# Encoder step on one core: the MLP as seven quarter products (one level of Strassen's algorithm) in place of the plain tiled product

## The chip, the core and the metric

The kernel runs on one core of a Trainium2 chip. TensorE (PE in the profile) multiplies, VectorE (DVE), ScalarE (ACT) and GpSimd (POOL) do elementwise work, and the queue of SyncE (SP) issues the transfers. The metric is the device time of one execution in microseconds, lower is better.

## The reference

Two post-norm layers are run over 1024 prompt rows and 32 sample rows, D = 1024, all in fp32. Each layer has attention, an output projection and then the MLP, the part that the change rewrites:

```python
x = layer_norm(ALPHA * x + g1 * (o @ w_out)) * ln1_g + ln1_b
u = layer_norm(x) * (1 + sc2) + sh2
f = jnp.square(jax.nn.relu(u @ w1)) @ w2        # w1 (1024, 4096), w2 (4096, 1024)
x = layer_norm(ALPHA * x + g2 * f) * ln2_g + ln2_b
```

## The kernel before

Activations lie transposed: features on the 128 partitions, the T = 1056 tokens along the free axis. TensorE is given fp32r operands: every fp32 operand x is split into hi = round(x) and lo = x - hi, and a product is three passes, hi·hi, lo·hi and hi·lo, added in PSUM (`three_pass`, L370).

The MLP of a layer runs in a block of its own (L2068). The 4096 hidden features are walked in 16 blocks of 256. `up` makes the two 128-row tiles of a block (8 depths x 3 passes x 3 column blocks of NB = 352), `down` multiplies the block before into all 8 output tiles (2 depths x 3 passes x 3 column blocks). That is 4608 matmuls of 352 columns for a layer. What the other engines do for a block of 256 features:

- POOL: `pool_split` (L349) makes hi (L356) and lo (L358) of two 1 MB weight chunks of 128x2048, and lo (L2083) of two hidden tiles of 128x1056.
- ACT: relu out of PSUM (L2136) and the rounded hidden tile (L2138), 128x1056, twice each.
- DVE: the square of a hidden tile (L2146), twice, and the scaled sum of each of 8 output tiles from PSUM into `acc` (L2163, three instructions a tile).

The first `up` block of a layer is fed while rows are turned: `turned_feed` (L423) transposes one depth at a time on TensorE, ACT scales and shifts it (`read_turned_rows`, L458), DVE splits it (`split_turned_rows`, L473: L496 hi, L498 lo) and TensorE multiplies it (L452). Ahead of the MLP block stands the block of the output projection and the first norm (L1922), behind it the block of the second norm (L922 or L2177): there `rows_back` (L814) turns `acc` back into rows (L821), and between its tiles the products for the next layer's conditioning run (`pe_chunks`, L603), whose first three weight chunks are loaded at the end of the MLP block. Engines meet at a barrier between blocks. Within a block each engine runs its own instruction list in order and waits on semaphores. `Own.settle` makes an engine wait for its own last instruction.

## Time and profile before

| what | value |
|---|---|
| median of 3 runs | 3213.33 us (3211.71 to 3226.49) |
| profiled execution, first to last instruction (the one time that its profile gives) | 3228.2 us |
| PE busy over the span | 2944.9 us, 91% |
| DVE busy | 1630.8 us, 51% |
| ACT busy | 871.7 us, 27% |
| POOL busy | 1514.3 us, 47% |
| mean granted TensorE clock | 0.930 |
| matmul instructions | 18646 |

A busy share says how long an engine had an instruction running, blocked ones included, averaged over stages that have different limits. Read it stage by stage. A matmul's listed duration overlaps its neighbours'; what one costs in a stream is the distance between starts.

### The profile page before, as it was taken

How to read it: one execution, taken by the hardware profiler on the slowest of the kernel's cores; microseconds unless marked ns; L12 is line 12 of the kernel's file. 1: busy time of each engine (PE TensorE's matmuls, PEld its weight loads, DVE VectorE, ACT ScalarE, POOL GpSimd, SP SyncE). 2: the span in 40 equal slices, each digit the busy share in tenths (PEclk: the TensorE clock that was granted, in tenths of full speed). 3: DMA queues.
4: the chain of work that ended last, by engine and by line, in shares of the span. 5: the costliest groups of instructions: out<-in, count | busy, mean ns of one | idle time of the engine just before them, and what ended most of it. 6: DMA issues, size and time to landing. Idle time of an engine off the chain costs nothing. (4 is left out here: it accounts for less than half of the span.)

```text
span 3228.2 us, 47279 instructions
## 1 busy us (share of the span) xinstructions
PE 2944.9 (91%) x18646; PEld 2808.2 (87%) x18646; DVE 1630.8 (51%) x3479; ACT 871.7 (27%) x1710; POOL 1514.3 (47%) x680
## 2 busy tenths in 40 slices
PE   5999899887999999999979989987979999999993
PEld 5999789565899999999979888985859999999993
DVE  6552688557423332333775418875654333333347
ACT  1331466325200010001253306663251110011001
POOL 2693596125334343444339727742334343434334
PEclk6999999889999999999779998997989999999996
DMA  5451211421111111110534412114211111111112
GB/s 227 161 170 54 79 41 44 140 90 71 66 40 52 39 52 39 52 39 26 214 144 157 159 37 58 45 39 151 95 65 40 53 39 52 39 51 39 52 40 94
DMA packets 117355, 253.65 MB, mean 79 GB/s; under 512 B 42565, under 2 KB 78953, under 8 KB 103701
## 3 DMA queue, kind: packets, MB, share of 16 engines
q1 hardware_dynamic: 110868, 228.58, 20.8%
q10 hardware_dynamic: 6336, 23.07, 2.0%
q8 instruction: 94, 1.54, 0.2%
q14 instruction: 57, 0.46, 0.0%
HBM read 217.19 MB, written 42.19 MB: 80 GB/s over the span
## 5 line engine op out<-in xcount | busy, mean ns | idle before, releaser
L377 PE MATMUL psum<-u_hi,w_hi 128*128 128x352 f32 x2016 | 651.4, 323 | 4.0 <-DVE v_rows L1240 4.0
L377 PE MATMUL psum<-u_lo,w_hi 128*128 128x352 f32 x2016 | 652.4, 324 | 0.0
L377 PE MATMUL psum<-u_hi,w_lo 128*128 128x352 f32 x2016 | 651.5, 323 | 0.0
L2163 DVE SCALAR_TENSOR_TENSOR acc_t<-psum,mods,acc_t 128x704 f32<-128x704 f32 x720 | 376.2, 578 | 275.0 <-PE psum L377 275.0
L377 PE MATMUL psum<-h_hi,w_lo 128*128 128x352 f32 x1536 | 495.3, 322 | 0.0
L377 PE MATMUL psum<-h_lo,w_hi 128*128 128x352 f32 x1536 | 495.0, 322 | 0.0
L377 PE MATMUL psum<-h_hi,w_hi 128*128 128x352 f32 x1536 | 494.3, 322 | 0.0
L356 POOL CAST w_hi<-w_raw 128x2048 fp32r<-128x2048 f32 x72 | 136.3, 1894 | 659.0 <-DVEq L2156 357.4
L2146 DVE TENSOR_TENSOR h_relu<-h_relu 128x1056 f32<-128x1056 f32 x64 | 112.2, 1753 | 634.3 <-ACT h_relu L2136 634.3
L377 PEld LDWEIGHTS psum<-u_hi,w_hi 128*128 128x128 f32 x2016 | 379.9, 188 | 5.2 <-issue 5.0
L377 PEld LDWEIGHTS psum<-u_lo,w_hi 128*128 128x128 f32 x2016 | 380.2, 189 | 0.0
L377 PEld LDWEIGHTS psum<-u_hi,w_lo 128*128 128x128 f32 x2016 | 379.6, 188 | 0.0
L2136 ACT ACTIVATE h_relu<-psum 128x1056 f32<-128x1056 f32 x64 | 67.4, 1052 | 1102.4 <-PE psum L377 1094.8
L358 POOL TENSOR_TENSOR w_lo<-w_raw,w_hi 128x2048 fp32r<-128x2048 f32 x72 | 359.0, 4986 | 5.8
L1067 POOL TENSOR_TENSOR ada_products<-w_ada_b,c_rows 128x1024 f32<-128x1024 f32 x88 | 238.5, 2742 | 128.6 <-DVE u_lo L498 97.2
L2083 POOL TENSOR_TENSOR h_lo<-h_relu,h_hi 128x1056 fp32r<-128x1056 f32 x64 | 158.1, 2471 | 283.0 <-ACT h_hi L2138 273.4
L377 PEld LDWEIGHTS psum<-h_hi,w_hi 128*128 128x128 f32 x1536 | 289.4, 188 | 0.0
L377 PEld LDWEIGHTS psum<-h_lo,w_hi 128*128 128x128 f32 x1536 | 289.1, 188 | 0.0
L377 PEld LDWEIGHTS psum<-h_hi,w_lo 128*128 128x128 f32 x1536 | 288.5, 188 | 0.0
L1474 PE MATMUL psum<-v_parts,probs_hi 128*128 128x128 f32 x840 | 204.3, 278 | 10.0 <-DVE o_head L1584 8.1
L1474 PE MATMUL psum<-v_parts,probs_lo 128*128 128x128 f32 x840 | 207.9, 282 | 0.0
L675 POOL TENSOR_TENSOR row_tiles<-row_tiles,ln_gain 128x1024 f32<-128x1024 f32 x32 | 76.1, 2377 | 249.5 <-ACT row_tiles L701 249.5
(267 smaller groups left out, 5724.0 us busy)
## 6 DMA issues: line engine op xcount, KB each, us to landing
w_raw<-in_w_all SPq DMA_DIRECT2D x86, 1024.0 KB, 4.8
w_ada_b<-in_w_ada_t ACTq DMA_DIRECT2D x44, 512.0 KB, 3.5
w_ada_v<-in_w_ada_t SPq DMA_DIRECT2D x20, 512.0 KB, 3.3
row_tiles<-in_x_prompt SPq DMA_DIRECT2D x16, 512.0 KB, 13.6
scr_o<-o_head SPq DMA_DIRECT2D x32, 256.0 KB, 2.6
row_tiles<-scr_o SPq DMA_DIRECT2D x16, 512.0 KB, 16.3
x_between_norms<-row_tiles SPq DMA_DIRECT2D x16, 512.0 KB, 2.6
mlp_rows<-x_between_norms SPq DMA_DIRECT2D x16, 512.0 KB, 6.9
```

The lines of the kernel that those rows point to most:

```text
L356: pool.tensor_copy(hi[:, 0:c], raw[s][:, 0:c]).then_inc(pool_step, 1)
L358: pool.tensor_tensor(lo[:, 0:c], raw[s][:, 0:c], hi[:, 0:c].bitcast(F32), ALU.subtract).then_inc(pool_step, 1)
L377: mm = pe.matmul(out[:, b, :], w[s][:, c:c + P], a[:, k, b * NB:(b + 1) * NB], start=(k == 0 and w is w_hi and a is a_hi), stop=(k == n - ...
L675: own.did(pool.tensor_tensor(x, x, ln_g[:], ALU.mult))
L1067: pool.tensor_tensor(ada_prod[c][:], ada_b[i % 2][:], c_rows[:, c, :], ALU.mult).then_inc(b_prod, 1)
L1474: mm = pe.matmul(psum[:, 6 + n % 2, 0:2 * HD], p[n % 2][:, b, :], v, start=(b == 0 and p is pt_hi), stop=(b == nb - 1 and p is pt_lo))
L2083: pool.tensor_tensor(h_lo[par][:, m, :], h_r[m][:], h_hi[par][:, m, :].bitcast(F32), ALU.subtract).then_inc(h_rdy, 1)
L2136: act.activation(h_r[m][:].rearrange("p (b c) -> p b c", c=NB), lin[m], ACT.Relu).then_inc(h_ev[m], 1)
L2146: dve.tensor_tensor(h_r[m][:], h_r[m][:], h_r[m][:], ALU.mult).then_inc(h_sqd, 1)
L2163: ins = dve.scalar_tensor_tensor(a, y, mods[:, 40 + m, c:c + 1], a, ALU.mult, ALU.add)
```

## The change

Both matrices of a layer's MLP are cut in 2x2 quarters, group by group: the hidden features are taken in SB = 4 groups of 1024. For a group, `up` is a product of a 1024x1024 piece of w1 with u and `down` one of a 1024x1024 piece of w2 with the hidden piece. Either is done as the seven products M1 to M7 of Strassen's algorithm, on 512x512 weight quarters and 512x528 token quarters. That makes 56 steps (`STEPS`), numbered g, a layer: `UP_ORDER` and `DOWN_ORDER` four times. A step has four output tiles m, each two column blocks of 264 x 4 depths x 3 passes: 96 matmuls of 264 columns. Operands that are sums of two quarters are summed in fp32 by DVE (`weight_sum`, `token_sum`), then rounded by ACT (`weight_high`, `token_high`); the rest is subtracted by POOL (`weight_low`, and `token_low` for depths 0 and 1) and by DVE (`token_low` for depths 2 and 3). Token parts are double buffered, half weight parts (index q = 2g, 2g+1) have three buffers. A sum shares its buffer with the low part that replaces it. A product's tile is added into one or two quarters of the hidden piece or of `acc`. The gate `g2` is applied once at the end of a layer (`gate`) and no longer in each sum. The weights are loaded as quarters of 1 MB, four a matrix.

The loads of the first two quarters stand in the block ahead, where POOL no longer splits the first chunk. `mlp_x` is now loaded behind the last `up` step, and the three conditioning chunks (`ada_r`) behind the last product. The diff, cut to its core and with leading blanks taken off (the transposes' `turn_depth` is as `turned_feed`'s, two PSUM pairs in turn; `evict` calls `evict_up` or `evict_down`; `gate` is four to six scaled copies of an output tile on ACT):

```diff
+SB = 4
+HT = KT // 2
+TH = 528
+NH2 = TH // 2
+UP_ORDER = ("M7", "M1", "M2", "M4", "M6", "M5", "M3")
+DOWN_ORDER = ("M2", "M4", "M5", "M3", "M7", "M1", "M6")
+PER = len(UP_ORDER)
+STEPS = [(s, half, name) for s in range(SB) for half, names in (("up", UP_ORDER), ("down", DOWN_ORDER)) for name in names]
+NSTEP = len(STEPS)
+CHAIN_HEAD = ("M7", "M2", "M5", "M6")
+WEIGHT_OF = {"M1": ((0, 0), (1, 1), 1), "M2": ((1, 0), (1, 1), 1), "M3": ((0, 0), None, 0), "M4": ((1, 1), None, 0),
+             "M5": ((0, 0), (0, 1), 1), "M6": ((1, 0), (0, 0), -1), "M7": ((0, 1), (1, 1), -1)}
+TOKEN_OF = {"M1": ((0, 0), (1, 1), 1), "M2": ((0, 0), None, 0), "M3": ((0, 1), (1, 1), -1), "M4": ((1, 0), (0, 0), -1),
+            "M5": ((1, 1), None, 0), "M6": ((0, 0), (0, 1), 1), "M7": ((1, 0), (1, 1), 1)}
...
-mlp_x = at("mlp_rows", U0, [P, NTT, D])
-ada_r = [at(f"w_ada_r{s}", U0 + 36864 + 8192 * s, [P, CW]) for s in range(3)]
+mlp_x = at("mlp_rows", W0 + 87040, [P, NTT, D])
+ada_r = [at(f"w_ada_r{s}", W0 + 53248 + 8192 * s, [P, CW]) for s in range(3)]
...
+m_raw = {q: at(f"w_quarter{i}", W0 + 8192 * i, [P, 2, D]) for i, q in enumerate(QUADS)}
+m_whi = [at(f"w_part_hi{s}", W0 + 32768 + 4096 * s, [P, D], F32R) for s in range(3)]
+lo_at = (W0 + 45056, W0 + 49152, Q0 + 83200)
+m_wlo = [at(f"w_part_lo{s}", o, [P, D], F32R) for s, o in enumerate(lo_at)]
+m_wsum = [at(f"w_part_sum{s}", o, [P, D]) for s, o in enumerate(lo_at)]
+m_thi = [at(f"token_part_hi{s}", W0 + 53248 + 16896 * s, [P, HT, TH], F32R) for s in range(2)]
+m_tlo = [at(f"token_part_lo{s}", W0 + 61696 + 16896 * s, [P, HT, TH], F32R) for s in range(2)]
+m_tsum = [at(f"token_part_sum{s}", W0 + 61696 + 16896 * s, [P, HT, TH]) for s in range(2)]
+m_u = at("mlp_in", W0 + 87040, [P, KT, T])
+m_h = at("mlp_hidden", Q0 + 40960, [P, KT, T])
+m_rest = at("mlp_rest", Q0 + 74752, [P, HT, TH])
...
-sp_weights(sp, l, UP0, 1)
+sp.wait_ge(raw_free, UP0 + 1)
+load_quarter(sp, l, 0, (1, 1))
+sp.wait_ge(raw_free, UP0 + 2)
+load_quarter(sp, l, 0, (0, 1))
...
-pool.wait_ge(f_last, USE + 1)
-pool_weights(pool, UP0, 1)
...
+sp.wait_ge(n_tlo_p, g + 1 + HT // 2 - 1)
+sp.wait_ge(n_tlo_v, g)
 mlp_rows_loaded(sp, 0, NTT)
 if l + 1 < DEPTH:
+    sp.wait_ge(n_mm, HT * NSTEP)
     sp_chunks(sp, l + 1, 0, 3)
...
+x = m_wsum[s][:] if b else m_raw[a][:, j, :]
+pool.wait_ge(n_whi, q + 1)
+pool.tensor_tensor(m_wlo[s][:], x, m_whi[s][:].bitcast(F32), ALU.subtract).then_inc(n_wlo, 1)
...
+pool.wait_ge(n_thi, g)
+pool.tensor_tensor(m_tlo[s][:, 0:2, :], x[:, 0:2, :], m_thi[s][:, 0:2, :].bitcast(F32), ALU.subtract)\
+    .then_inc(n_tlo_p, 1)
...
+for g in range(1, NSTEP):
+    if g == 1:
+        weight_low(2)
+        token_low(1)
+    else:
+        token_low(g)
+        weight_low(2 * g)
+    weight_low(2 * g + 1)
...
+def product(g, m):
+    name = STEPS[g][2]
+    first = name in CHAIN_HEAD
+    if m == 0:
+        pe.wait_ge(n_tlo_p, g + HT)
+        if g > 0:
+            pe.wait_ge(n_tlo_v, g)
+    if m % 2 == 0:
+        pe.wait_ge(n_wlo, 2 * g + m // 2 + 1)
+    if g > 0:
+        if ACT_EV[g] > ACT_EV[g - 1]:
+            pe.wait_ge(n_eva, HT * ACT_EV[g - 1] + m + 1)
+        if DVE_EV[g] > DVE_EV[g - 1]:
+            pe.wait_ge(n_evv, HT * DVE_EV[g - 1] + m + 1)
+    s, w = parity(g), half_slot(2 * g + m // 2)
+    for b in range(2):
+        for k in range(HT):
+            c = 256 * k + P * (m % 2)
+            for a, t in ((m_whi, m_thi), (m_wlo, m_thi), (m_whi, m_tlo)):
+                mm = pe.matmul(banks(m)[:, b, :], a[w][:, c:c + P], t[s][:, k, NH2 * b:NH2 * b + NH2],
+                               start=(first and k == 0 and a is m_whi and t is m_thi),
+                               stop=(k == HT - 1 and t is m_tlo), skip_group_check=not first)
+    mm.then_inc(n_mm, 1)
...
+for i in range(6):
+    turn_depth(i)
+product(0, 0)
+turn_depth(6)
+pe.wait_ge(n_rows, 1)
+product(0, 1)
+turn_depth(7)
+pe.wait_ge(n_feed, 8)
+product(0, 2)
+product(0, 3)
...
+act.activation(m_thi[parity(g)][:], x, ACT.Copy).then_inc(n_thi, 1)
...
+func = ACT.Copy if name in ("M7", "M1") else ACT.Relu
+own.did(act.activation(split_two(out), banks(m), func), n_eva)
+if func is ACT.Relu:
+    own.settle()
+    own.did(act.activation(out, out, ACT.Square), n_sq)
...
+for g in range(1, NSTEP):
+    if g >= 2:
+        evict(g - 2, 3)
+    token_high(g)
+    if g >= 2:
+        weight_high(2 * g)
+    evict(g - 1, 0)
+    evict(g - 1, 1)
+    weight_high(2 * g + 1)
+    evict(g - 1, 2)
+for m in range(HT):
+    gate(m)
...
+def weight_sum(q):
+    g, j = q // 2, q % 2
+    a, b, sign = WEIGHT_OF[STEPS[g][2]]
+    if not b:
+        return
+    quarters_ready(dve, g)
+    if q >= 3:
+        dve.wait_ge(n_mm, HT * ((q - 3) // 2) + 2 * ((q - 3) % 2) + 2)
+    own.did(dve.tensor_tensor(m_wsum[half_slot(q)][:], m_raw[a][:, j, :], m_raw[b][:, j, :],
+                              ALU.add if sign > 0 else ALU.subtract), n_wsum)
+def token_sum(g):
+    s, half, name = STEPS[g]
+    a, b, sign = TOKEN_OF[name]
+    if not b:
+        return
+    if g >= 2:
+        dve.wait_ge(n_mm, HT * (g - 1))
+    if half == "down":
+        own.settle()
+        dve.wait_ge(n_sq, 2 * HT * s + (HT if name == "M4" else 2 * HT))
+    x = source(g)
+    own.did(dve.tensor_tensor(m_tsum[parity(g)][:], quarter_of(x, a), quarter_of(x, b),
+                              ALU.add if sign > 0 else ALU.subtract), n_tsum)
...
+dve.wait_ge(n_thi, g)
+own.did(dve.tensor_tensor(m_tlo[s][:, 2:4, :], x[:, 2:4, :], m_thi[s][:, 2:4, :].bitcast(F32),
+                          ALU.subtract), n_tlo_v)
...
+def accumulate(dst, m, op, first, done):
+    if first:
+        ins = dve.tensor_copy(split_two(dst), banks(m))
+    else:
+        own.settle()
+        ins = dve.tensor_tensor(split_two(dst), split_two(dst), banks(m), op)
+    own.did(ins, done)
+def relu_square(x, done):
+    own.settle()
+    own.did(dve.scalar_tensor_tensor(x, x, 0.0, x, ALU.max, ALU.mult), done)
+def evict_up(g, m, s, name):
+    h11, h22 = piece_of(m_h, (0, 0), m), piece_of(m_h, (1, 1), m)
+    if name == "M7":
+        return
+    dve.wait_ge(n_mm, HT * g + m + 1)
+    if name in ("M1", "M4", "M3"):
+        dve.wait_ge(n_eva, HT * ACT_EV[g] + m + 1)
+    if name == "M1":
+        own.did(dve.tensor_tensor(split_two(h22), banks(m), split_two(h22), ALU.subtract), n_evv)
+    elif name == "M2":
+        accumulate(h11, m, ALU.subtract, False, None)
+        accumulate(h22, m, ALU.subtract, False, n_evv)
+    elif name == "M4":
+        accumulate(h11, m, ALU.add, False, n_evv)
+    elif name == "M6":
+        accumulate(h22, m, ALU.add, False, n_evv)
+    elif name == "M5":
+        accumulate(h11, m, ALU.subtract, False, None)
+        accumulate(h22, m, ALU.subtract, False, n_evv)
+        relu_square(h11, n_hid)
+    elif name == "M3":
+        accumulate(h22, m, ALU.add, False, n_evv)
+        relu_square(h22, n_hid)
...
+def finish(m):
+    y11, y12, y21, y22 = (piece_of(acc, q, m) for q in ((0, 0), (0, 1), (1, 0), (1, 1)))
+    own.settle()
+    own.did(dve.tensor_tensor(y11, y11, y22, ALU.subtract))
+    own.settle()
+    own.did(dve.tensor_tensor(y22, y11, y12, ALU.add))
+    own.did(dve.tensor_tensor(y11, y11, y21, ALU.add))
+    own.settle()
+    own.did(dve.tensor_tensor(y22, y22, m_rest[:, m, :], ALU.subtract), n_fin)
...
+accumulate(piece_of(acc, y[name], m), m, ALU.add, s == 0 and name != "M5", n_evv)
+if name == "M1" and s == SB - 1:
+    finish(m)
...
+for g in range(1, NSTEP):
+    if g >= 2:
+        evict(g - 2, 3)
+    token_sum(g)
+    if g >= 2:
+        weight_sum(2 * g)
+    evict(g - 1, 0)
+    token_low(g)
+    evict(g - 1, 1)
+    weight_sum(2 * g + 1)
+    evict(g - 1, 2)
+evict(NSTEP - 2, 3)
+for m in range(HT):
+    evict(NSTEP - 1, m)
```

## Rows read from the trace of the kernel before

**Rows 1.** granted clock and busy time by stretch, first MLP block

```profile
core 0: us, PE busy (x) PEld busy (x) DVE busy (x) ACT busy (x) POOL busy (x), PEclk, DMA share, GB/s
...
1000.00:1200.00 200.00, 200.00 (x1252) 200.00 (x1251) 65.24 (x106) 20.33 (x19) 79.90 (x27) 1.00 0.13 45
1570.00:1650.00 80.00, 65.46 (x328) 64.93 (x326) 73.38 (x128) 47.51 (x92) 50.40 (x20) 0.52 0.45 160
```

**Rows 2.** timeline, both ends of the first MLP block

```profile
start us, us, engine line op out<-in xcount [idle before <-releaser]
...
808.69 1.03 PE L428 MATMUL psum<-ident,row_tiles 32*128 32x32 f32 x8 [19.88 <-PEq L1922]
...
812.30 1.20 ACT L468 ACTIVATE turned_tile<-psum,mods 128x1024 f32<-128x1024 f32 x1 [2.17 <-PE psum L435]
...
1566.59 1.57 DVE L2163 SCALAR_TENSOR_TENSOR acc_t<-psum,mods,acc_t 128x704 f32<-128x704 f32 x3 [1.42 <-PE psum L377]
...
1569.74 4.48 PE L821 MATMUL psum<-ident,acc_t 128*128 128x128 f32 x24 [3.30 <-PEq L2175]
```

**Rows 3.** timeline of PE, 258-column matmuls, first and last of 48

```profile
155.46 0.28 PE L1112 MATMUL psum<-w_hi,u_hi 128*128 128x258 f32 x1
...
161.08 0.28 PE L1112 MATMUL psum<-w_lo,u_hi 128*128 128x258 f32 x1
```

**Rows 4.** groups by line and form of DVE, POOL, ACT, 900 to 1500

```profile
L2163 DVE SCALAR_TENSOR_TENSOR acc_t<-psum,mods,acc_t 128x704 f32<-128x704 f32 x104 | 98.7, 949 | 118.0 <-PE psum L377 118.0
L2163 DVE SCALAR_TENSOR_TENSOR acc_t<-psum,mods,acc_t 128x320 f32<-128x320 f32 x104 | 56.4, 542 | 0.0
...
L358 POOL TENSOR_TENSOR w_lo<-w_raw,w_hi 128x2048 fp32r<-128x2048 f32 x27 | 136.4, 5052 | 2.2
L2083 POOL TENSOR_TENSOR h_lo<-h_relu,h_hi 128x1056 fp32r<-128x1056 f32 x26 | 64.2, 2470 | 112.1 <-ACT h_hi L2138 107.9 <-POOL w_lo L358 4.2
...
L2138 ACT ACTIVATE h_hi<-h_relu 128x1056 fp32r<-128x1056 f32 x26 | 28.3, 1089 | 44.3 <-DVE h_relu L2146 44.3
```

**Rows 5.** timeline, DVE and POOL at 1059 to 1065

```profile
1049.07 1.26 DVE L2146 TENSOR_TENSOR h_relu<-h_relu 128x1056 f32<-128x1056 f32 x1 [10.94 <-ACT h_relu L2136]
1060.67 2.01 DVE L2146 TENSOR_TENSOR h_relu<-h_relu 128x1056 f32<-128x1056 f32 x1 [10.35 <-ACT h_relu L2136]
1062.61 1.56 DVE L2163 SCALAR_TENSOR_TENSOR acc_t<-psum,mods,acc_t 128x704 f32<-128x704 f32 x3
...
1059.68 1.89 POOL L356 CAST w_hi<-w_raw 128x2048 fp32r<-128x2048 f32 x1 [5.69 <-ACTq L2135]
1061.65 5.53 POOL L358 TENSOR_TENSOR w_lo<-w_raw,w_hi 128x2048 fp32r<-128x2048 f32 x1
```

**Rows 6.** timeline, DVE, POOL and PE at 817 to 841

```profile
817.53 1.23 DVE L498 TENSOR_TENSOR u_lo<-turned_tile,u_hi 128x1024 fp32r<-128x1024 f32 x1
...
834.20 4.85 POOL L358 TENSOR_TENSOR w_lo<-w_raw,w_hi 128x2048 fp32r<-128x2048 f32 x1
...
834.70 5.43 DVE L498 TENSOR_TENSOR u_lo<-turned_tile,u_hi 128x1024 fp32r<-128x1024 f32 x1
...
840.19 0.66 PE L452 MATMUL psum<-u_hi,w_hi 128*128 128x352 f32 x1 [3.85 <-DVE u_lo L498]
...
840.94 0.49 PE L452 MATMUL psum<-u_lo,w_hi 128*128 128x352 f32 x1
```

**Rows 7.** granted clock in the same place

```profile
840.00:843.00 3.00, 2.81 (x10) 2.81 (x10) 1.97 (x3) 0.00 (x0) 0.00 (x0) 0.50 0.89 292
```

**Rows 8.** timeline, a norm's tile, POOL and ACT

```profile
740.07 2.40 POOL L675 TENSOR_TENSOR row_tiles<-row_tiles,ln_gain 128x1024 f32<-128x1024 f32 x1 [2.92 <-ACT row_tiles L701]
...
735.63 1.06 ACT L708 ACTIVATE row_products<-row_tiles 128x1024 f32<-128x1024 f32 x1
...
736.82 0.20 ACT L710 ACTIVATE row_figures<-row_figures 128x1 f32<-128x1 f32 x1
```

**Rows 9.** DMA issues of the page: KB each, us to landing

```profile
w_ada_r<-in_w_ada_k SPq DMA_DIRECT2D x8, 1024.0 KB, 7.1
```

289 lines of the change are left out of this document (185 added, 104 removed).

## The prediction

> **What bounds the kernel now.** I read the table of slices on the page first: PE is busy nearly all the time in two long plateaus at full clock, the MLP blocks of the two layers. The stretch table shows what such a plateau is: in 200 us PE starts 1252 matmuls, has no idle time and is granted 1.00, its 2.4 GHz level, while DVE is busy 65, ACT 20 and POOL 80 of 200 us [rows 1]. So a matmul of 352 columns costs 200/1252 = 159.7 ns, and nothing but their number sets the pace. The timeline gives the block's ends: 808.7 us, first transpose, to 1569.7 us, first transpose of the next block [rows 2], 761 us. Of them 4608 x 0.1597 = 736 are matmuls; some 25 are the turning of rows at the start and the drain and barrier at the end. A cheaper product can gain here, as long as the three other engines keep their hidden place. That they do now is because they have little to do: the question is what they must do for each product afterwards, and whether they may do it at the same time.
>
> **PE's part of the change.** 56 steps x 96 = 5376 matmuls of 264 columns a layer, 7/8 of the columns. Is a column as cheap in the shorter form? The nearest row is the V projection with 258 columns, new weights for each matmul as here: 48 starts from 155.46 to 161.08, 47 distances, 119.6 ns [rows 3], 0.463 ns a column where 352 columns have 0.454. 264 columns lie between 119.8 (by the second) and 122.4 (by the first); I take 122. A step is then 96 x 0.122 = 11.7 us (a tile m 2.93) and a layer 56 x 11.7 = 656 us, 80 less than 736. If nothing else bound, that would be the gain, 160 us in all.
>
> **What the others must do in a step of 11.7 us.** Durations by the nearest rows:
> - POOL, `token_low` of 2x528: 2.47 as L2083's 1056; each of two `weight_low` of 1024: between 2.25 (half of L358's 4.5 when nothing holds it up, below) and 2.40 (L675); I take 2.35 [rows 4, 8]. Together 7.2 in every step.
> - DVE, reading two SBUF tiles: `weight_sum` of 1024 1.23 (L498), `token_low` of 1056 1.26 (L2146), `token_sum` of 2112 2.36 (1.26 and 1056 more at 1.04 ns), a relu-square of 528 0.71 [rows 5, 6].
> - DVE, one operand in PSUM: an eviction of 528, between L2163's 0.54 for 320 and 0.95 for 704, 0.76, and 0.80 with `settle` [rows 4].
> - ACT: `weight_high` 1.06, `token_high` of 2112 0.20 + 2 x 0.89 = 1.97 (at most 2.18 as two of L2138), a copy of 528 out of PSUM 0.64 [rows 4, 8].
>
> Sums by engine, over the 14 steps of a group of features: DVE 20 weight sums, 10 token sums, 14 low parts, 8 squares and 28 + 32 evictions, some 118 us or 8.4 a step; POOL 7.2; ACT some 6. Each is under 11.7. By busy shares alone the change works.
>
> **But DVE and POOL don't run side by side.** At 834.20 POOL begins a `w_lo` that takes 4.85 to 839.05. DVE's L498, 1.23 elsewhere, begins at 834.70 and takes 5.43: to 840.13, 1.08 after POOL's end. PE waited 3.85 us for it [rows 6]. At 1060.67 DVE's square takes 2.01 and ends 1.1 after POOL's cast; POOL's L358, issued right behind the cast, takes 5.53, 4.5 of it after DVE's end at 1062.68: the waiting DVE goes first. Yet L2163, with an operand in PSUM, runs its normal 1.56 in the middle of that L358 [rows 5]. So a DVE instruction with two SBUF inputs and a POOL instruction exclude each other for their whole length, a waiting one gets its turn as the other ends, and it is then 0.15 shorter. The squares are of a form (`scalar_tensor_tensor`) that [rows 5] show only with a PSUM operand; I count them as excluding, by L2146, which reads two SBUF inputs too. Not excluding, they would take 4.5 us off 14 steps, 0.3 a step and 35 in all. The Trainium skill (SBUF — State Buffer, Who interferes with whom) goes by inputs and not by form: any VectorE instruction with two SBUF inputs and a GpSimd one that reads SBUF block each other fully. By that rule the squares count and the 35 us stay in; L498, L2146 and L358 agree with it.
>
> Before, this cost little: 80 us of POOL and some 20 of squares in 200. Now nearly all new work is of the excluding kind. A step with both sums has POOL 7.2 + DVE 2.2 + 2 x 1.08 + 1.1 (the blocked lengths) = 12.7; six of 14 steps are such, four have weight sums only (10.5) and four token sums only (10.5), and the squares add 4.5: 165 us in 14 steps, 11.8 a step if never one moment were lost. That already equals PE's 11.7.
>
> **And moments are lost**, since each engine keeps its order. In a step with both sums this is a chain, each link waiting for the one before: `token_sum` 2.2, `token_high` 1.97, POOL's `token_low` 2.47, DVE's `token_low` 1.1, first `weight_low` 2.35 (here the next product may start), second `weight_sum` 1.08 (it stood in DVE's list behind `token_low` and then behind POOL's instruction), `weight_high` 1.06, second `weight_low` 2.35, which the next `token_sum` meets and waits out: 14.6, with eight handovers of 0.05 15.0 us. Taking DVE's half of `token_low` first, steps of 11.9 and 16.2 alternate, mean 14.0. The other steps, followed engine by engine in program order, from the start of M1 on: M2 11.8, M4 15.9 (M2's eight evictions stand ahead), M6 12.7, M5 13.8, M3 15.2, then M2 14.8, M4 18.6 (M3's evictions and squares, each waiting for ACT and POOL), M5 12.9, M3 12.2, M7 12.6, M1, M6, M7, M1 15.0 each. Sum 200.5, **14.3 us a step**, PE idle a fifth of it.
>
> **The ends of a block.** Start: 808.7 to the first feed 812.3 as before [rows 2]. Six depths are turned before a product, 2 us each while cold, then sum, rounding and low part by depth on DVE and POOL: product 0 at about 822.4; two tiles, two more depths, `n_feed` 8 at 831.5; then `token_sum` 2.4, `token_high` 2.0, both low parts in turn 3.7: product 1 at 839.8, 31.1 us in. End: the last step has `finish`, four two-SBUF instructions a tile (3 us), one ahead of its `token_low`, so 3 more before it, and the rest delay its second weight half, `gate` and last sums: 18 us from its start to the end of DVE's work, and 1.6 to the next block. Layer: 31.1 + 3 x 200.5 + (200.5 - 30.0) + 3 + 18 + 1.6 = 826 against 761: **+65**. Break-even is a step of (761 - 31 - 23)/54 = 13.1.
>
> **The rest.** The chunk split taken from POOL at the end of the block ahead ended before ACT's last norm there: 0. The weights are the same bytes, in quarters asked for two to three steps (over 25 us) ahead, the tightest some 9 us ahead, and a 1 MB load takes 7.1 with others beside it: 0, or a stall of a few us where a quarter is late. `mlp_x` comes seven steps early: 0. The conditioning chunks now start with the last product instead of seven loads earlier; the first is wanted 4 us into the next block and takes 7.1 [rows 9], so about 3 once, in a block in which PE is bound at half clock [rows 1]. Bounds of this part, 0 and 15.
>
> **The sum.** 2 x 65 + 3 = +133 on the profiled execution's 3228 gives 3361; that execution lies 15 above the median of the runs, 3213, from which I get **3346**. I give 3345.
>
> **The clock.** After its 3.85 us of idling PE stood at 0.50, the 1.2 GHz level, for some 3 us, 352 columns at 0.29 us each [rows 6, 7]. Steps here leave PE idle for 2 to 4 us, so a product may lose 1.6 us again at each start. I cost that at nothing: the port chain (15.0) is longer than the slowed product (13.3), the two overlap. Without that cover it is 54 x 1.6 x 2 = 170.
>
> **Rivals.**
> - A, as above: 13.5 to 15.1 us a step by other turns at the port, 3260 to 3435.
> - B, the turns fall better and the chain overlaps with the next step: 11.9 to 13.1 us, mean 12.6; 3345 - 108 x 1.7 = 3161, faster. It decides below 13.1. For it: the port's pure sum is 11.8. Against: the orders are fixed and ACT's rounding, 3 us a step, leaves the port unused.
> - C, exclusion doesn't matter and PE stays the bound, 11.7 us: 3345 - 108 x 2.6 = 3064. Against it: [rows 5, 6]. The skill's page TensorE: Matmul & The Clock Gate (Back-to-back issue gap) gives N/2.4 + 2.5 ns, 112.5 for 264 columns; by that this case would be some 100 us lower, but 258 columns took 119.6 where it says 110.
> - D, the half clock reaches the path, because stalls and slow products follow each other: up to +170, say 3450 to 3520. For it: [rows 7]. Against: the stall hides it.
> - E, near balance (13.0 to 13.2 us): 3205 to 3226.
>
> **Chances and range.** A 0.66, B 0.13, C 0.08, D 0.10, E 0.03. Slower by over 0.5% (about what a measurement of this kernel can tell from no change): A and D and the rest, 0.77; within 0.5% 0.04; faster 0.19. The range 3130 to 3460 takes in A, most of B, E and the lower end of D; it leaves out C and D's top. A's own range is 3260 to 3435.
>
> **What will show it.** In the MLP blocks of the changed kernel: matmuls of 264 columns 120 to 122 ns apart within a product; PE idle 2 to 4 us ahead of most products, released by POOL's `weight_low` or DVE's `token_low`; DVE's two-SBUF groups well above their unblocked length (`weight_sum` mean 1.7 or more, not 1.23) and their ends just behind POOL's; steps of 14 to 15 us; PE's busy share down to 80 to 85%. Wrong if products follow each other without a gap (C), if matmuls stand 0.22 us apart in most of the block (D), or if the step is under 13.1 though PE waits (B).

## The result, and the profile after

The changed kernel takes 3284.22 us (median of 4), the one before beside it on the same chip 3214.99 us (median of 4): ratio 1.0208, interval 1.0184 to 1.0232, **slower by 2.1%, 69 us**. The forecast was 3345 us, slower by 132. The profiled execution took 3290.36 us, its span 3288.5.

Busy time and share of each engine, and the table of slices, from the page of the changed kernel:

```profile
PE 2842.8 (86%) x20182; PEld 2693.0 (82%) x20182; DVE 2325.7 (71%) x3567; ACT 1302.4 (40%) x2156; POOL 1907.5 (58%) x830
...
PE   5999899787889899898879998987969898989983
...
PEclk6999989888999999999769999997989999999996
```

PE is still the busiest by far (86%), and its row in the MLP plateaus shows eights and nines where solid nines stood before. The same stretches as in [rows 1], the columns as there:

```profile
1000.00:1200.00 200.00, 181.52 (x1419) 179.69 (x1418) 161.13 (x118) 69.76 (x67) 130.19 (x45) 0.96 0.13 46
1614.68:1698.26 83.58, 66.13 (x329) 65.63 (x329) 74.97 (x136) 49.05 (x94) 50.35 (x20) 0.52 0.47 172
```

In 200 us there are 1419 shorter matmuls instead of 1252, and PE is idle for 18.5 us of them; POOL's busy time went from 80 to 130, DVE's from 65 to 161. The stretch behind the block, with the conditioning chunks, is as long as before (83.6 us against 1652.93 - 1569.74 = 83.2). The ends of the block and its first two products, timeline of PE:

```profile
818.01 0.28 PE L2193 MATMUL psum<-ident,row_tiles 32*128 32x32 f32 x1 [16.98 <-PEq L1964]
...
835.17 0.59 PE L2224 MATMUL psum<-token_part_hi,w_part_hi 128*128 128x264 f32 x1 [7.80 <-POOL token_part_lo L2177]
...
854.21 0.39 PE L2224 MATMUL psum<-token_part_hi,w_part_hi 128*128 128x264 f32 x1 [1.86 <-POOL token_part_lo L2171]
...
1614.68 0.45 PE L858 MATMUL psum<-ident,acc_t 128*128 128x128 f32 x1 [5.30 <-PEq L2466]
```

The block lasts 1614.68 - 818.01 = 796.67 us, where [rows 2] had 761.05: +35.6. In the second layer it is 795.66 against 762.24: +33.4. Both together, 69.0, equal the difference of the medians. In part that is chance: the two profiled executions differ by 60.3 us (3288.5 - 3228.2), so outside the blocks this one was 9 us shorter; the last section comes back to that. Product 1 comes 36.2 us in; from it to the start of step 55 there are 740.5 us, 54 steps of 13.71; the end takes 19.95.

What sets the step is seen in the groups by form, 1000 to 1600 us (mean ns of one; then idle time before and what ended it):

```profile
L2224 PE MATMUL psum<-token_part_hi,w_part_hi 128*128 128x264 f32 x1397 | 410.7, 294 | 60.1 <-POOL w_part_lo L2164 51.9 <-DVE token_part_lo L2355 4.6 <-issue 3.5
...
L2333 DVE TENSOR_TENSOR w_part_sum<-w_quarter,w_quarter 128x1024 f32<-128x1024 f32 x63 | 134.3, 2132 | 2.1 <-PE psum L2224 2.1
L2363 DVE TENSOR_TENSOR mlp_hidden<-mlp_hidden,psum 128x528 f32<-128x528 f32 x84 | 59.1, 704 | 36.3 <-ACT mlp_hidden L2284 26.1 <-PE psum L2224 5.1
L2355 DVE TENSOR_TENSOR token_part_lo<-token_part_sum,token_part_hi 128x1056 fp32r<-128x1056 f32 x32 | 58.3, 1821 | 12.3 <-ACT token_part_hi L2274 11.8
...
L2368 DVE SCALAR_TENSOR_TENSOR mlp_hidden<-mlp_hidden 128x528 f32<-128x528 f32 x24 | 23.5, 977 | 0.8
L2355 DVE TENSOR_TENSOR token_part_lo<-mlp_in,token_part_hi 128x1056 fp32r<-128x1056 f32 x6 | 19.4, 3230 | 0.0
...
L2164 POOL TENSOR_TENSOR w_part_lo<-w_part_sum,w_part_hi 128x1024 fp32r<-128x1024 f32 x63 | 189.7, 3017 | 69.1 <-ACT w_part_hi L2260 69.1
L2171 POOL TENSOR_TENSOR token_part_lo<-token_part_sum,token_part_hi 128x1056 fp32r<-128x1056 f32 x32 | 105.8, 3306 | 118.8 <-ACT token_part_hi L2274 118.8
...
L2171 POOL TENSOR_TENSOR token_part_lo<-mlp_in,token_part_hi 128x1056 fp32r<-128x1056 f32 x6 | 14.8, 2471 | 5.4 <-ACT token_part_hi L2274 5.4
```

Most of PE's idle time was ended by POOL's `weight_low` (51.9 of 60.1 us). `weight_sum` takes 2.13 us in the mean, and 1.22 when nothing holds it (the run with POOL's work cut, below). An eviction with an operand in PSUM takes 0.704 us with or without POOL. The two halves of `token_low` show the turns: without a token sum (`mlp_in`) POOL begins first, takes 2.47, its plain length, and DVE's takes 3.2. With a token sum it is mixed, 1.8 in the mean for DVE and 3.3 for POOL: of the ten such steps in 14, DVE begins first in six and takes its plain 1.26. In the other four POOL has begun before DVE was free, as for the product M1 of `down` (the first two rows). The rows behind them are of the next step, M6. Timeline of DVE, POOL, ACT and PE:

```profile
1190.12 2.73 DVE L2355 TENSOR_TENSOR token_part_lo<-token_part_sum,token_part_hi 128x1056 fp32r<-128x1056 f32 x1
1188.27 3.46 POOL L2171 TENSOR_TENSOR token_part_lo<-token_part_sum,token_part_hi 128x1056 fp32r<-128x1056 f32 x1
...
1197.89 4.07 DVE L2347 TENSOR_TENSOR token_part_sum<-mlp_hidden 128x2112 f32<-128x2112 f32 x1
1201.88 1.21 DVE L2333 TENSOR_TENSOR w_part_sum<-w_quarter,w_quarter 128x1024 f32<-128x1024 f32 x1
...
1204.00 1.26 DVE L2355 TENSOR_TENSOR token_part_lo<-token_part_sum,token_part_hi 128x1056 fp32r<-128x1056 f32 x1
1205.37 0.70 DVE L2363 TENSOR_TENSOR acc_t<-acc_t,psum 128x528 f32<-128x528 f32 x1
1205.99 2.68 DVE L2333 TENSOR_TENSOR w_part_sum<-w_quarter,w_quarter 128x1024 f32<-128x1024 f32 x1
...
1204.05 3.54 POOL L2171 TENSOR_TENSOR token_part_lo<-token_part_sum,token_part_hi 128x1056 fp32r<-128x1056 f32 x1 [4.30 <-ACT token_part_hi L2274]
1207.54 3.34 POOL L2164 TENSOR_TENSOR w_part_lo<-w_part_sum,w_part_hi 128x1024 fp32r<-128x1024 f32 x1
...
1201.99 1.98 ACT L2274 ACTIVATE token_part_hi<-token_part_sum 128x2112 fp32r<-128x2112 f32 x1 [4.71 <-DVE token_part_sum L2347]
...
1211.14 0.36 PE L2224 MATMUL psum<-token_part_hi,w_part_hi 128*128 128x264 f32 x1 [3.45 <-POOL w_part_lo L2164]
```

In M6's step both low halves are released by the same `token_high` (ended 1203.97). DVE starts 0.05 us before POOL and takes its plain 1.26 us; POOL's runs 1.0 longer than alone and ends at 1207.59. DVE's `weight_sum`, begun at 1205.99, takes 2.68 instead of 1.22 and ends 1.08 behind POOL. So turns alternate as forecast, but in this step DVE has the first one.

Followed from its start, this chain is `token_sum` 4.07, `token_high` 1.98, POOL's low half 3.54, `weight_low` 3.34, and the product starts 13.25 us after the sum did. The same instructions take 2.36, 2.47 and 2.42 where nothing holds them (the runs with POOL's or DVE's work short, below). At those lengths the chain would be 3.7 us shorter, 9.55: an estimate, but well below the 11.65 us that the matmuls of a step take (measured below). Without the held time this chain alone would not have made PE wait.

### The profile page after: what moved, and what is told of

Same layout as the page of the kernel before. It is cut to its first block and busy times, and to the rows that moved or that the text cites. A ratio compares the mean times of both kernels' runs of the same rounds, so it can differ in the third digit from the quotient of the medians.

```text
span 3288.5 us, 50721 instructions
## 1 busy us (share of the span) xinstructions
PE 2842.8 (86%) x20182; PEld 2693.0 (82%) x20182; DVE 2325.7 (71%) x3567; ACT 1302.4 (40%) x2156; POOL 1907.5 (58%) x830
## 5 line engine op out<-in xcount | busy, mean ns | idle before, releaser
L2224 PE MATMUL psum<-token_part_hi,w_part_hi 128*128 128x264 f32 x3584 | 1054.9, 294 | 171.4 <-POOL w_part_lo L2164 131.1
L2224 PE MATMUL psum<-token_part_hi,w_part_lo 128*128 128x264 f32 x3584 | 1045.6, 292 | 0.0
L2224 PE MATMUL psum<-token_part_lo,w_part_hi 128*128 128x264 f32 x3584 | 1045.2, 292 | 0.0
L2224 PEld LDWEIGHTS psum<-token_part_hi,w_part_hi 128*128 128x128 f32 x3584 | 703.1, 196 | 186.3 <-issue 161.2
L2224 PEld LDWEIGHTS psum<-token_part_hi,w_part_lo 128*128 128x128 f32 x3584 | 703.6, 196 | 0.0
L2224 PEld LDWEIGHTS psum<-token_part_lo,w_part_hi 128*128 128x128 f32 x3584 | 703.4, 196 | 0.0
L2164 POOL TENSOR_TENSOR w_part_lo<-w_part_sum,w_part_hi 128x1024 fp32r<-128x1024 f32 x160 | 472.9, 2961 | 229.4 <-ACT w_part_hi L2260 229.4
L400 PE MATMUL psum<-u_hi,w_hi 128*128 128x352 f32 x576 | 186.9, 325 | 4.3 <-DVE v_rows L1277 4.3
L400 PE MATMUL psum<-u_lo,w_hi 128*128 128x352 f32 x576 | 186.8, 324 | 0.0
L400 PE MATMUL psum<-u_hi,w_lo 128*128 128x352 f32 x576 | 186.6, 324 | 0.0
## 6 DMA issues: line engine op xcount, KB each, us to landing
row_tiles<-in_x_prompt SPq DMA_DIRECT2D x16, 512.0 KB, 13.7
```

The costliest lines, as they stand in the source:

```text
L400: mm = pe.matmul(out[:, b, :], w[s][:, c:c + P], a[:, k, b * NB:(b + 1) * NB], start=(k == 0 and w is w_hi and a is a_hi), stop=(k == n - ...
L2164: pool.tensor_tensor(m_wlo[s][:], x, m_whi[s][:].bitcast(F32), ALU.subtract).then_inc(n_wlo, 1)
L2224: mm = pe.matmul(banks(m)[:, b, :], a[w][:, c:c + P], t[s][:, k, NH2 * b:NH2 * b + NH2], start=(first and k == 0 and a is m_whi and t is m ...
```

## The experiments

Three theories were tried. T: a DVE instruction with two SBUF inputs and a POOL instruction exclude each other, and their sum in turn sets the step. R: DVE has too much to do whatever POOL does. C: there is no exclusion, but POOL's 2.4 us instructions lie in the chain from a sum to its product. All runs have the changed kernel as their basis. Means of a step are those of 14 steps of a full group of features; in the changed kernel 191.24 us from 1033.16, 13.66 a step (191.1 to 191.2 in each of its four full groups). A single run of this kernel can lie some 12 us to either side of another one, by what the last section shows.

**POOL's part short**

```diff
-pool.tensor_tensor(m_wlo[s][:], x, m_whi[s][:].bitcast(F32), ALU.subtract).then_inc(n_wlo, 1)
+n = 32 if g >= PER else KT * P
+pool.tensor_tensor(m_wlo[s][:, 0:n], x[:, 0:n], m_whi[s][:, 0:n].bitcast(F32), ALU.subtract)\
+    .then_inc(n_wlo, 1)
...
-pool.tensor_tensor(m_tlo[s][:, 0:2, :], x[:, 0:2, :], m_thi[s][:, 0:2, :].bitcast(F32), ALU.subtract)\
+n = 16 if g >= PER else TH
+pool.tensor_tensor(m_tlo[s][:, 0:2, 0:n], x[:, 0:2, 0:n], m_thi[s][:, 0:2, 0:n].bitcast(F32), ALU.subtract)\
...
+if g >= PER:
+    a, t = m_whi, m_thi
```

> GpSimd's part taken away. From the second group of hidden features on (42 of the 56 steps of a layer), weight_low and token_low on POOL do 32 of 1024 and 16 of 264 columns, and the matmuls of these steps read the high parts in the low parts' place (as many, of the same shape); everything on DVE and ACT is as in the changed kernel. The output is left wrong by that. Theory T (a DVE instruction with two SBUF inputs and a POOL instruction shut each other out, so that their sum sets the step): the step falls from the measured 13.7 to 11.7 to 12.1 us, the rate of 96 matmuls of 0.1216 us, the median of weight_sum falls from 2.09 to 1.21 us and that of token_sum from 2.7 to 2.35 us; the whole 3284 - 2 x 42 x 1.8 = about 3133 us. Rival R (DVE simply has too much to do, whatever POOL does): the step stays at 13.7 us, the whole at 3284. Rival C (no exclusion, but POOL's 2.4 us instructions lie in the chain from the sums to the matmuls): the step falls too, so this run alone does not tell T from C; the durations of weight_sum and the next runs do.

The condition `g >= PER` makes the work short from step 7 on, in 49 of 56 steps a layer and not in 42 as the expectation says: by its own price the whole should be 3284 - 2 x 49 x 1.8 = 3108. Measured: 3068.62 us (one run). That is 39 below even this, for a good part since the steps fell by 2.0 and not by 1.8, and the end of a block by 2 as well. The MLP blocks went from 796.7 and 795.7 us to 691.8 and 692.6, 49 steps x 2.0 being 98 of the 105 and 103. Of the table of stretches:

```profile
1000.00:1400.00 400.00, 400.00 (x3298) 400.00 (x3297) 271.68 (x276) 172.11 (x168) 49.48 (x103) 1.00 0.16 58
```

and of its groups the one of `weight_sum`:

```profile
L2339 DVE TENSOR_TENSOR w_part_sum<-w_quarter,w_quarter 128x1024 f32<-128x1024 f32 x49 | 59.9, 1223 | 12.9 <-PE psum L2230 12.9
```

PE has no idle time: 3298 matmuls in 400 us, 121.3 ns each, so 11.65 us a step. `weight_sum` is 1.22 where it was 2.13. R is wrong: DVE's work was untouched and the step fell to the matmuls' rate.

**DVE's two-input work short**

```diff
+n = 32 if g >= PER else KT * P
+own.did(dve.tensor_tensor(m_wsum[half_slot(q)][:, 0:n], m_raw[a][:, j, 0:n], m_raw[b][:, j, 0:n],
...
+n = 8 if g >= PER else TH
+own.did(dve.tensor_tensor(m_tsum[parity(g)][:, :, 0:n], quarter_of(x, a)[:, :, 0:n],
+                          quarter_of(x, b)[:, :, 0:n],
...
+n = 16 if g >= PER else TH
+own.did(dve.tensor_tensor(m_tlo[s][:, 2:4, 0:n], x[:, 2:4, 0:n], m_thi[s][:, 2:4, 0:n].bitcast(F32),
```

> The mirror of the run before: POOL works at full length, and of DVE the instructions with two SBUF inputs are short from the second group of hidden features on (weight_sum 32 of 1024 columns, token_sum 8 of 528, token_low 16 of 264 of the two depths); ACT and POOL then read the first quarter in the place of the sum, and the matmuls the high parts in the place of the low ones. DVE's evictions stay. The output is left wrong by that. Theory T: the step falls to 11.7 to 12.1 us and POOL's instructions all take their 2.36 to 2.48 us, none 3.5 or 4.5; the whole about 3133 us. Rival R (DVE's own amount): the same. Rival C (POOL's latency in the chain): the step stays above 13 us, the whole at 3230 or more. T alone lets both this run and the one with POOL short fall to the matmuls' rate.

Measured: 3109.49 us (one run); again from step 7 on. A step is 12.0 us in the mean of a full group: 11.65 in eleven of 14, but 11.9, 14.7 and 13.1 around the start of `down`, where the squares, still at full length, and the evictions of M3 lie. Stretch, then groups of POOL and DVE:

```profile
1000.00:1400.00 400.00, 394.30 (x3231) 393.58 (x3231) 199.69 (x265) 169.76 (x165) 243.94 (x101) 1.00 0.14 49
```

```profile
L2164 POOL TENSOR_TENSOR w_part_lo<-w_quarter,w_part_hi 128x1024 fp32r<-128x1024 f32 x68 | 164.3, 2422 | 35.6 <-ACT w_part_hi L2262 35.6
L2171 POOL TENSOR_TENSOR token_part_lo<-mlp_in,token_part_hi 128x1056 fp32r<-128x1056 f32 x19 | 47.2, 2485 | 64.3 <-ACT token_part_hi L2276 64.3
...
L2336 DVE TENSOR_TENSOR w_part_sum<-w_quarter,w_quarter 128x32 f32<-128x32 f32 x49 | 37.0, 755 | 20.6 <-PE psum L2226 20.6
```

POOL does its full work, each instruction at its plain 2.42 to 2.49 us, and PE is idle 5.7 of 400 us. With POOL's instructions in the chain at full length the step fell all the same, which C had put at over 13 us. By itself that does not refute C, because the short sums shorten the chain from sum to product too. With the lengths it does: weight sums at 1.22 instead of 2.13 in the run before, and the chain above at 9.55 us without the held time. The last row shows the exclusion from the other side: a sum of 32 columns, 0.19 us where POOL is short as well, takes 0.76 in the mean beside POOL. DVE's work alone fits under the product, POOL's alone nearly does, and the two together do not: T.

**Both short**

The edits of both runs together.

> Both together: POOL's instructions and DVE's with two SBUF inputs short from the second group of hidden features on, with the matmuls, ACT's high parts and DVE's evictions as they are (the matmuls read the high parts in place of the low ones, so the output is left wrong). What is left is the matmuls' own rate and the evictions. All theories on the operands: steps of 11.7 us and the whole 3284 - 2 x 42 x 2.0 = about 3116 us. If the steps stay at 12.5 us or above, evictions, the clock or the matmuls' rate hold a part of the 2 us that I put down to the operands. Half clock in the steps would show here as steps of over 13 us.

Measured: 3072.12 us (one run), `token_high` 11.67 us apart. An MLP block is 688 us; the two runs above come within 5 and 24 us of that. The granted clock from 1000 to 1400 us is 1.00.

**All low parts on DVE**

POOL's list behind the first step is gone:

```diff
-own.did(dve.tensor_tensor(m_tlo[s][:, 2:4, :], x[:, 2:4, :], m_thi[s][:, 2:4, :].bitcast(F32),
-                          ALU.subtract), n_tlo_v)
+own.did(dve.tensor_tensor(m_tlo[s][:], x[:, :, :], m_thi[s][:].bitcast(F32), ALU.subtract), n_tlo_v)
...
+dve.wait_ge(n_whi, q + 1)
+own.did(dve.tensor_tensor(m_wlo[s][:], x, m_whi[s][:].bitcast(F32), ALU.subtract), n_wlo)
...
 token_low(g)
+if g >= 2:
+    weight_low(2 * g)
 evict(g - 1, 1)
 weight_sum(2 * g + 1)
 evict(g - 1, 2)
+weight_low(2 * g + 1)
```

> Every low part behind the first step is made by DVE (weight_low two of 1.2 us, token_low one of 2.35 us instead of half of it), and POOL does nothing in the steps. The computation is complete. Theory T: POOL's 7.3 us a step no longer shut DVE out; DVE's work without waits is 8.4 us a step in the mean (1.8 weight sums, 1.7 token sums, 1.2 token lows, 3.7 evictions) and gets 3.6 us more, 12.0, so a step is 12.0 to 12.7 us against 13.7, and the whole 3284 - 2 x 53 x (1.0 to 1.7) = 3104 to 3178 us: faster than the kernel before. Rival R (DVE's amount sets the step, no exclusion): DVE has more to do, the step gets longer by 3.6 us to 17 us and the whole 3650 us. Rival C (POOL's latency in the chain): also shorter, 12 to 13 us; the run with DVE short tells C from T.

Measured: 3196.5 us, ratio to the kernel before 0.9909 (0.9876 to 0.9942). By the ratios that is 2.9% faster than the changed kernel, with one engine less at work. One period of 14 steps, then DVE's groups:

```profile
1007.34:1186.20 178.86, 167.98 (x1345) 166.90 (x1345) 156.46 (x141) 68.25 (x66) 0.00 (x0) 0.98 0.13 48
```

```profile
L2354 DVE TENSOR_TENSOR w_part_lo<-w_part_sum,w_part_hi 128x1024 fp32r<-128x1024 f32 x46 | 56.2, 1221 | 7.5 <-ACT w_part_hi L2251 7.5
L2324 DVE TENSOR_TENSOR w_part_sum<-w_quarter,w_quarter 128x1024 f32<-128x1024 f32 x46 | 56.1, 1219 | 0.0
L2346 DVE TENSOR_TENSOR token_part_lo<-token_part_sum,token_part_hi 128x2112 fp32r<-128x2112 f32 x23 | 54.2, 2357 | 9.9 <-ACT token_part_hi L2265 9.1
```

178.86 us, 12.78 a step. DVE is busy for 156 us of them, hardly more than in the changed kernel (152, much of it held up), although it does POOL's part as well: 3.6 us a step where POOL took 7.2, and every instruction at its plain length. R forecast 17 us a step. T's forecast was too good as well: 12.0 to 12.7 us a step and at most 3178 us, and both came out above, the whole by 18 us. C had forecast 12 to 13 us here too; against it stand the lengths.

**POOL first, and DVE first**

```diff
 dve.wait_ge(n_thi, g)
+dve.wait_ge(n_tlo_p, g + HT)
```

> The changed kernel with one wait more: DVE's half of token_low waits until POOL's half of the same step is made, so POOL always goes first. The computation is complete. In the changed kernel DVE took its half first in the steps with token sums (its instruction there took 1.26 us, POOL's 3.5), and steps of 11.8 and 15.3 us alternated in the M7, M1 and M6 stretch, 54.1 us for four, where the prediction had 15.0 each, 60.0. Theory T (exclusion; my sum per step was right and only my choice of who goes first was wrong): these four steps become 15.0 us each, the period of 14 steps 191.6 + 6 to 9 = 198 to 201 us, and the whole 3284 + 2 x 3.8 x (6 to 9) = 3330 to 3352 us, the predicted 3345. Rival (the turn does not matter, the sum was too high for another reason): the steps stay at 13.7 us in the mean and the whole at 3284.

Measured: 3399.53 us (one run), 14 steps in 205.89 us, 14.71 a step; the stretch from M7 to M1 has four steps of 15.69, 15.73, 15.68 and 15.70. From M1 to M2 it was 11.76 and from M2 to M4 14.91 (in three of the eight groups 13.3 and 13.4, the same sum). Timeline:

```profile
1213.73 2.46 POOL L2171 TENSOR_TENSOR token_part_lo<-token_part_sum,token_part_hi 128x1056 fp32r<-128x1056 f32 x1 [4.30 <-ACT token_part_hi L2274]
1216.15 2.39 POOL L2164 TENSOR_TENSOR w_part_lo<-w_part_sum,w_part_hi 128x1024 fp32r<-128x1024 f32 x1
...
1216.30 3.37 DVE L2356 TENSOR_TENSOR token_part_lo<-token_part_sum,token_part_hi 128x1056 fp32r<-128x1056 f32 x1 [2.71 <-POOL token_part_lo L2171]
```

The turn matters, by more than expected: DVE's wait lets go only when POOL has ended, and POOL has by then begun its next instruction, `weight_low`. So POOL has two turns running, and DVE's low half, begun at 1216.30, takes 3.37 us. The forecast 15.0 had DVE's half ahead of `weight_low`; how much of the 0.7 us above it comes from this other order was not separated. The whole is 47 us above the top of T's range: besides the four steps (62.8 against 54.1) the four from M4 to the end of `up` grew from 53.7 to 59.9 us, which the expectation had left as they were.

```diff
 pool.wait_ge(n_thi, g)
+pool.wait_ge(n_tlo_v, g)
```

> The changed kernel with the opposite order forced: POOL's half of token_low waits until DVE's half of the same step is made. The computation is complete. In the changed kernel DVE went first by itself in the steps with token sums and POOL first in the others, where DVE's half took 3.2 us. Theory (the turn costs, not the wait as such): the steps M7, M1, M6, M7 stay at 54 us for the four, the period of 14 at 190 to 194 us against 191.6, and the whole at 3284, between 3265 and 3300; with POOL first it was 206 us and 3400. Rival (any more wait between the two engines costs, whichever way round): the period grows here as well, to 198 us or more, and the whole to 3330 or more.

Measured: 3305.22 us (one run), 14 steps in 194.31 us, the four steps from M7 on 13.48, 13.47, 13.47 and 12.55, together 53.0. By the period this lies just outside what the theory gave (190 to 194), by the time 5 us above it. The expectation's premise, that DVE goes first by itself in all steps with token sums, holds for six of ten in the trace. The stretch with token sums is no longer than in the changed kernel (54.1), as the theory said; what it costs lies elsewhere, in `up`, M2 to M4 taking 12.86 and M4 to M6 15.82 where they took 12.12 and 12.54. The rival's 198 was not reached. Both orders forced cost time, DVE first 3 us a period and POOL first 15.

**token_high in halves**

```diff
-act.activation(m_thi[parity(g)][:], x, ACT.Copy).then_inc(n_thi, 1)
+for k in (0, 2):
+    act.activation(m_thi[parity(g)][:, k:k + 2, :], x[:, k:k + 2, :], ACT.Copy).then_inc(n_thi, 1)
...
-pool.wait_ge(n_thi, g)
+pool.wait_ge(n_thi, 2 * g - 1)
...
-dve.wait_ge(n_thi, g)
+dve.wait_ge(n_thi, 2 * g)
```

> ACT makes token_high in two halves of the depths; POOL's half of token_low waits for the first alone, DVE's for both. The computation is complete. Between token_sum and the low parts neither DVE nor POOL works on SBUF while ACT takes 1.97 us; now POOL starts about 1.0 us earlier, and it goes first. Theory T: the stretch without use of the port gets 1 us shorter in the steps with a token sum, but POOL first costs what DVE first saved, so a step is 13.2 to 14.3 us and the whole between 3250 and 3320 us. If only the length of the chain from sum to matmul counted (no exclusion), it would be 1 us off every step with a token sum: 3284 - 2 x 53 x 10 / 14 x 1.0 = about 3208 us.

Measured: 3253.32 us (one run), 14 steps in 187.96 us, 13.43 a step. Inside T's span, and far from the 3208 of a mere chain: 1 us less of unused port gives back 0.23 us a step. POOL's half starts first in every step here; that this turn eats the rest is argued and not shown apart.

**ACT's evictions earlier**

The version with all low parts on DVE, and on ACT, behind M4 and M3 of `up`:

```diff
+early = STEPS[g - 1][1:] in (("up", "M4"), ("up", "M3"))
+if early:
+    evict(g - 1, 0)
+    evict(g - 1, 1)
 token_high(g)
 if g >= 2:
     weight_high(2 * g)
-evict(g - 1, 0)
-evict(g - 1, 1)
+if early:
+    evict(g - 1, 2)
+else:
+    evict(g - 1, 0)
+    evict(g - 1, 1)
 weight_high(2 * g + 1)
-evict(g - 1, 2)
+if not early:
+    evict(g - 1, 2)
```

> The version with all low parts on DVE, and on ACT one order changed: in the steps behind M4 and M3 of the upper half, the eviction of products 0 and 1 comes ahead of token_high, and that of product 2 ahead of the second weight_high. The computation is complete. In the trace of the version before it DVE stood idle 2.4, 2.5 and 1.7 us in every 14 steps because ACT's eviction of the same product sat behind token_high and weight_high, which waited for DVE's sums. Theory: these 6.6 us of 178.9 go, steps of 15.3, 15.0 and 16.1 us become 12.9, 12.6 and 14.4, the mean 12.3 us; the whole 3196 - 2 x 3.8 x 6.6 = 3146 us, range 3140 to 3170. Rival (DVE's work alone sets those steps, the idle time is slack): no change, 3196 us.

The idle time it is aimed at, in the version without it, DVE and ACT:

```profile
1055.22 0.70 DVE L2361 TENSOR_TENSOR mlp_hidden<-mlp_hidden,psum 128x528 f32<-128x528 f32 x1 [2.40 <-ACT mlp_hidden L2275]
...
1051.72 1.97 ACT L2265 ACTIVATE token_part_hi<-token_part_sum 128x2112 fp32r<-128x2112 f32 x1 [9.33 <-DVE token_part_sum L2338]
1053.60 1.04 ACT L2251 ACTIVATE w_part_hi<-w_part_sum 128x1024 fp32r<-128x1024 f32 x1
1054.55 0.59 ACT L2275 ACTIVATE mlp_hidden<-psum 128x528 f32<-128x528 f32 x1
```

DVE waits 2.40 us for an eviction of ACT that stands behind 3 us of other work, though its product had been there. Measured with the new order: 3137.45 us, ratio 0.9737 (0.9712 to 0.9761), 14 steps in 173.22 us, 12.37 a step; the three steps are 13.15, 13.05 and 14.59, each 0.2 to 0.5 above the forecast. The time is 3 us below the forecast range: the two MLP blocks together are 56 us shorter, where 50 were forecast.

**Two weight_low a group back on POOL**

DVE leaves these two out:

```diff
+for g in range(2, NSTEP):
+    if STEPS[g][1:] in (("up", "M4"), ("up", "M3")):
+        pool.wait_ge(n_wlo, 2 * g + 1)
+        weight_low(2 * g + 1)
```

> The same, and POOL makes one weight_low in each of the steps behind M4 and M3 of the upper half, where DVE has most to do. The computation is complete. POOL takes 2.4 us for what DVE does in 1.2, and while it does, DVE can only evict. Theory T: DVE's evictions, 0.7 us each, cover at most half of the 2.4 us, so the gain is 0 to 1 us in two of 14 steps: 3146 - 2 x 3.8 x (0 to 2) = 3131 to 3146 us, and a loss of the same size where DVE's next sum stands against POOL. Without exclusion it would be 1.2 us in each of the two steps at least, 18 us in all.

Measured: 3134.15 us, ratio 0.9728 (0.9711 to 0.9744), 14 steps in 173.10 us instead of 173.22. The interval overlaps that of the run before: POOL's help is worth nothing that can be measured.

**The first step's low part on DVE**

```diff
 own.did(dve.tensor_copy(m_thi[0][:, i, :], m_tsum[0][:, i, :]), n_hid)
+own.settle()
+own.did(dve.tensor_tensor(m_tlo[0][:, i, :], m_tsum[0][:, i, :],
+                          m_thi[0][:, i, :].bitcast(F32), ALU.subtract), n_tlo_p)
```

> The version with all low parts on DVE but two a group, and ACT's early evictions; in addition the first step's token_low, four pieces of 528 columns, is made by DVE behind its sum and cast of each piece instead of by POOL. The computation is complete. In the trace DVE's cast took 1.42 us beside POOL and 0.43 alone, and a sum up to 2.1; four pieces of 0.71 + 0.43 + 0.71 us are 7.4 us from 809.2, 816.6, against product 0 at 821.1. Theory T: product 0 comes 3 to 4 us earlier a layer, the whole 3134 - 6 to 8 = 3127 us, range 3122 to 3134. Rival (the transposes or ACT set the start): no change.

The rows behind it, from the changed kernel's start, DVE and POOL:

```profile
824.02 0.43 DVE L2442 CAST token_part_hi<-token_part_sum 128x528 fp32r<-128x528 f32 x1
...
825.11 1.43 DVE L2442 CAST token_part_hi<-token_part_sum 128x528 fp32r<-128x528 f32 x1
...
824.54 1.71 POOL L2177 TENSOR_TENSOR token_part_lo<-token_part_sum,token_part_hi 128x528 fp32r<-128x528 f32 x1 [1.57 <-DVE token_part_hi L2442]
```

A cast of 528, with a single SBUF input, takes 0.43 us alone and 1.43 beside POOL, ending 0.29 behind it. Measured: 3126.78 us, ratio 0.9742 (0.9713 to 0.9771), an interval too wide to tell 7 us. The traces tell it: product 0 comes 14.8 us into the block instead of 17.2, so 2.4 us earlier (forecast 3 to 4), and the blocks take 720.4 and 720.0 us where the version before took 722.4 and 724.0.

**Halves again, now without POOL**

```diff
+dve.wait_ge(n_thi, 2 * g - 1)
+own.did(dve.tensor_tensor(m_tlo[s][:, 0:2, :], x[:, 0:2, :], m_thi[s][:, 0:2, :].bitcast(F32),
+                          ALU.subtract))
+dve.wait_ge(n_thi, 2 * g)
+own.did(dve.tensor_tensor(m_tlo[s][:, 2:4, :], x[:, 2:4, :], m_thi[s][:, 2:4, :].bitcast(F32),
+                          ALU.subtract), n_tlo_v)
```

with `token_high` in halves as above.

> The same with token_high and token_low each made in two halves of the depths, so that DVE's first low half starts when ACT's first high half is there. The computation is complete. DVE stood idle for 1.2 us between token_sum, its eviction and token_low in the steps with a token sum; that goes to 0.2. It counts only where DVE, not the matmuls, sets the step (four to five of 14): 4 to 5 us of 173, so the whole is 3127 - 2 x 3.8 x 4 to 5 = 3089 to 3097 us. Against it: one more instruction of some 0.1 us a step. If the idle time is slack of ACT's own chain and not DVE's, no change: 3127 us.

Measured: **3099.72 us, ratio to the kernel before 0.9644 (0.9626 to 0.9661)**, 14 steps:

```profile
994.11:1162.01 167.90, 164.31 (x1346) 163.70 (x1345) 155.37 (x152) 69.87 (x80) 4.80 (x2) 1.00 0.14 51
```

167.90 us, 11.99 a step, PE idle 3.6 of them. It is 27 us faster than the version without the halves on the same chip (forecast 30 to 38), 3.6% faster than the kernel before, and by the ratios 5.5% faster than the changed one. In the mean of the four full groups the halves took 3.0 us off a period where POOL took part (191.2 to 188.2) and 3.3 here (172.3 to 169.0; forecast 4 to 5).

## Why the prediction was right, and what it mis-sized

The sum, term by term; the effect is that on the difference of the two layers together:

| term | forecast | measured | effect on the time |
|---|---|---|---|
| start to product 1, a layer | 31.1 | 36.2 and 35.6 | +10 |
| 54 steps from there, a layer | 775 (14.3 each) | 740.5 (13.71 each) | -69 |
| last step and end, a layer | 19.6 | 19.95 | +1 |
| clock | 0 | contained in the steps, see below | |
| conditioning chunks, once | 3 | 0.4 | -3 |

That makes 133 + 10 - 69 + 1 - 3 = 72. Measured are 69.0 for the two blocks and 0.4 for the chunks; 1.2 us of what is left is the second block of before, longer by that than the first (762.24), and the rest rounding.

The direction held by 0.66 us a step over the break-even of 13.05 ((761 - 36.2 - 20)/54), where the forecast had 1.2; the change is half of what was forecast. The step was missed by 0.6, as much as that margin, so that the sign came out right has some luck in it.

**The mechanism** was right: DVE's instructions with two SBUF inputs and POOL's take turns, and the chain of those turns is longer than a product. Matmuls of 264 columns stand 121.3 ns apart where nothing holds them (forecast 122). The Trainium skill (TensorE: Matmul & The Clock Gate, Back-to-back issue gap) gives N/2.4 + 2.5 ns for an isolated matmul; 112.5 for 264 columns, worked out from it, is too low for this stream, and the measurement decides. By busy shares every engine has room, and the two runs in which DVE or POOL has no two-input work fall to the matmuls' rate or near it, while the run that takes POOL away entirely and loads DVE with its work is faster than both kernels. The runs without the exclusion (3068.62 and 3072.12) came close to case C's price, 3064; part of that is chance, as seven steps a layer were left whole in them and the start was 5 us longer than priced. The squares count as excluding: beside POOL they took 0.98 us in the mean in the changed kernel, 0.71 without it. The Trainium skill's rule (SBUF — State Buffer, Who interferes with whom) that two SBUF inputs decide and not the form agrees with that. The Trainium skill's other rule there, that whoever asks first holds the pair to the end of its instruction, agrees with the timeline at 1204.00. Two signs did not come as forecast. PE should have been idle 2 to 4 us ahead of most products and for a fifth of the time; it is idle 1.9 us or more ahead of four products of 14 (1.9, 2.9, 6.6 and 3.5 us) and for a tenth of the time (18.5 of 191.2 us). Its share is 86%, not 80 to 85.

**The term that was mis-sized is the step, 14.3 us.** Over a period of 14 the forecast intervals sum to 200.5, measured 191.2. The difference lies mainly in three places. The last four, to M1, M6, M7 and M1 again, were put at 15.0 each, 60.0; they took 11.77, 15.29, 13.26 and 13.75, 54.1: -5.9. The interval from M2 to M4 of `up` was put at 15.9 and took 12.1: -3.8. That from M1 to M2 was put at 11.8 and took 13.3: +1.5. The other eight, 112.8, took 111.8, with single misses of up to 1.5 us either way.

For the first place the working used one order for every step, POOL's half of `token_low` first. The trace has neither that nor the alternative it names, "Taking DVE's half of `token_low` first, steps of 11.9 and 16.2 alternate, mean 14.0": the first turn itself alternates, POOL's in the steps of M1 of `down` and M7 of `up` (by 1.8 us), DVE's in those of M6 and M1 of `up` (by 0.05 us). The mean is 13.5. The two forced orders show that the turn moves the step by this much, and also that the prices were only near: with POOL first the four took 62.8 (forecast 60.0), with DVE first 53.0 (by the alternative 56). With POOL first the other two places moved to the forecast's side as well, in five of eight groups to 14.9 and 11.8. How much of the 9.3 us is due to the turn alone stays open, since each added wait changed more than the turn.

**The start** was 5 us too short, for two reasons. Product 0 came 17.2 us in and not 13.7: I had DVE's cast of 528 at its plain length, and it was held for a microsecond three times out of four, one sum for 2.1 us besides (2.86 instead of 0.70); the version with that low part off POOL got 2.4 us back. And product 0 with the turning of two depths took 19.0 us and not 17.4: behind 7.8 us in which PE was idle its first 19 matmuls stood 0.22 us apart, 1.9 us in all ahead of the last two transposes, for which the chain to product 1 waits. The granted clock of the first 6 us was 0.66, part of them at the 1.2 GHz level:

```profile
835.17:841.50 6.33, 6.33 (x37) 6.33 (x38) 0.00 (x0) 0.31 (x1) 2.31 (x1) 0.66 0.00 0
```

**The clock** was costed at nothing in the steps because the port chain hides it. In a period PE is idle for 18.5 us of 191.2, and 14 x 11.65 = 163.1 are the products; most of the remaining 9.7 us is four products a period that begin with 16 to 23 matmuls 0.22 us apart, at the 1.2 GHz level: M1 and M3 of `up`, M4 and M6 of `down`, which lose 1.6, 1.6, 2.4 and 1.6 us. Each of the four stands behind 1.9 to 6.6 us of idle time. Stretch tables, first the product M4 of the changed kernel, then two successive groups of the version with early evictions:

```profile
1144.91:1158.98 14.07, 14.07 (x97) 14.07 (x97) 6.79 (x6) 2.12 (x2) 9.84 (x4) 0.82 0.00 1
```
```profile
999.87:1173.09 173.22, 166.48 (x1345) 165.40 (x1345) 156.71 (x141) 68.62 (x66) 0.00 (x0) 0.99 0.14 49
1173.09:1344.76 171.67, 164.97 (x1344) 163.88 (x1345) 156.61 (x141) 68.62 (x66) 0.00 (x0) 1.00 0.14 50
```

Whether such a loss reaches the time depends on the place. In the run with POOL first, M1 and M2 together take 26.67 us whether M1 begins slow (13.26 and 13.41) or not (11.76 and 14.91): the stall hides it, as the prediction said. In the version with early evictions the two groups differ in M4's interval alone, 13.29 against 11.74, and by the same 1.5 us as a whole: there it is on the path. In the changed kernel M4's interval, with no idle time behind it, is its matmuls and nothing else. If the loss counts there, it is up to 2.4 us a period, some 18 us in all (an estimate), and the chain of turns is worth that much less; no run separates it. The 170 us of case D did not come. These 1.5 us are also why single periods of the later versions must be compared with care.

**B** was the rival on the other side: steps of 11.9 to 13.1. The step came 0.6 us above its bound. The fixed orders and ACT's rounding kept it there, as argued; halving the rounding alone gave 13.43, still not enough.

**The rest** was as forecast: a quarter of 1 MB took 4.8 us to land (median), no wait of PE in a step was ended by a DMA, and the stretch between the blocks is unchanged.

## What to carry to other kernels

Work that is put on two engines which exclude each other must be added up, not laid side by side: POOL's 7.2 us a step cost more than they relieved, and giving DVE the same work in half the time made a slower change into one that is faster than the kernel before, by 0.9% at once and 3.6% after four more edits, one of which gained nothing. When such a step is costed by hand, the order of turns counts beside the durations (13.7, 13.9 or 14.7 us a step here), and it need not be the same in every step; price both and keep both in the range. Once the shared resource is free, look for the next wait of the same engine: earlier evictions on ACT and the halving of one rounding and its low part were worth 56 and 28 us in the MLP blocks.

## What the runs showed of the hardware

A cast with one SBUF input is held by POOL too (0.43 us alone, 1.43 beside it), while an addition with one operand in PSUM is not (0.702 us without POOL, 0.704 with it). The Trainium skill lists casts among those that can take the shared pair (SBUF — State Buffer, Who interferes with whom), which I had not applied to the start; the trace agrees.

The work ahead of the first MLP block is the same code in the changed kernel and in all runs built on it, yet that block begins at 818.0 us in the changed kernel and at 816.4 in the run with both short, and between 802.9 and 805.2 in the ten others. Stretch tables of the changed kernel and of the one with DVE first, in the attention stage:

```profile
400.00:450.00 50.00, 46.08 (x272) 42.57 (x272) 38.09 (x132) 27.14 (x81) 38.50 (x32) 0.76 0.14 39
```
```profile
400.00:450.00 50.00, 45.19 (x350) 41.77 (x350) 45.51 (x160) 34.39 (x98) 46.62 (x39) 1.00 0.15 41
```

At 400 us the one starts 272 matmuls at a granted clock of 0.76, the other 350 at 1.00, in the same code. What decides it is open. It fits that single runs of one kernel lie some 12 us apart, and it is why a term here is read from the MLP blocks, which agree within 4 us between the two layers of each execution, and not from the whole time.
